# Two down projections as seven half products in three slices, with eight modulation rows made in the mixers before them

## The reference

```python
D_MODEL = 1024; SEQ = 256; D_FF = 2816

def _swiglu(xn, w_gate, w_up, w_down):
    g = jnp.einsum('bsd,df->bsf', xn, w_gate)
    up = jnp.einsum('bsd,df->bsf', xn, w_up)
    return jnp.einsum('bsf,fd->bsd', jax.nn.silu(g) * up, w_down)

# first block, for each layer
h = _swiglu(_rmsnorm(x, pre_ffn_g[layer]), ffn_w_gate[layer], ffn_w_up[layer], ffn_w_down[layer])
x = x + _rmsnorm(h, post_ffn_g[layer])

# second block, layer l: twelve rows of 512 columns each, of which the first four
# (shift and scale of the first norm) are in layer 0 also wanted for the context's condition
m = jnp.split(silu_c @ w_ada[l] + b_ada[l], 6, axis=-1)
csh1, csc1, cg1, csh2, csc2, cg2 = jnp.split(silu_cc @ w_ada[l] + b_ada[l], 6, axis=-1)
```

## Time and profile before

| | us |
|---|---|
| median of three runs | 1881.2 (1881.18 to 1881.66) |
| profiled execution, its own time | 1880.99 |
| its span, first to last instruction | 1879.2 |
| granted TensorE clock, mean | 0.992 |
| TensorE busy | 1821.9 (97%) |
| VectorE busy | 657.0 (35%) |
| ScalarE busy | 376.0 (20%) |

### The profile page before, as it was taken

One profiled execution on the slowest core, in us unless ns is written; L12 is line 12 of the kernel. 1 busy time (PEld: TensorE's weight loads), 2 busy tenths in 40 slices (PEclk: granted clock), 3 DMA queues, 4 the chain that ended last, 5 costly groups with the idle time before them and its releaser, 6 DMA issues.

```text
span 1879.2 us, 24366 instructions
## 1 busy us (share of the span) xinstructions
PE 1821.9 (97%) x10194; PEld 1200.2 (64%) x10196; DVE 657.0 (35%) x1353; ACT 376.0 (20%) x831; POOL 15.4 (1%) x31
## 2 busy tenths in 40 slices
PE   8999999999999999999999998999999999998998
PEld 7799988857999888575444433335885444433333
DVE  3278876432678653533111110112233111110112
ACT  3441110322311103423211110112013211111111
POOL 1000000000000100000000000000000000000000
PEclk9999999999999999999999999999999999999999
DMA  9744686732356883349999999999568999999996
GB/s 301 241 179 171 272 336 286 293 121 90 135 234 258 336 327 141 129 177 343 427 426 423 434 429 432 434 425 425 225 235 308 420 427 423 432 433 430 432 427 265
DMA packets 54323, 595.81 MB, mean 317 GB/s; under 512 B 6096, under 2 KB 20688, under 8 KB 24656
## 3 DMA queue, kind: packets, MB, share of 16 engines
q1 hardware_dynamic: 53648, 592.29, 76.9%
q10 hardware_dynamic: 576, 2.10, 0.3%
HBM read 588.90 MB, written 1.05 MB: 314 GB/s over the span
## 4 chain that ended last, share of the span: by engine, by line
PE 77%; DMA 19%; DVE 3%; ACT 1%; issue 0%; SPq 0%; DVEq 0%; ACTq 0%
PE ps L1357 18%; DMA ring<-in_w_up 17%; PE ps L568 16%; PE ps L870 8%; PE ps L785 7%; PE ps L1487 7%; PE ps L1312 3%; DMA ring<-in_w_ff_up 2%; PE ps L1305 2%; PE ps L638 2%; PE ps L924 1%; PE ps L727 1%; PE ps L656 1%; PE ps L670 1%; PE ps L1126 1%; PE ps L1086 1%
## 5 line engine op out<-in xcount | busy, mean ns | idle before, releaser
L1357 PE MATMUL ps<-ring,work 128*64 128x512 f32 x1792 | 405.8, 607 | 34.9 <-DMA ring<-in_w_up 29.6
L1357 PEld LDWEIGHTS ps<-ring,work 128*64 128x64 f32 x1792 | 128.8, 140 | 300.3 <-issue 248.2
L1804 ACT ACTIVATE work<-ps 128x512 f32<-128x512 f32 (+1 forms) x167 | 87.9, 532 | 696.2 <-PE ps L1487 248.7
L568 PE MATMUL ps<-hsq,ring 128*128 128x256 f32 x1024 | 225.1, 381 | 0.8 <-DVE hsq L2270 0.8
L568 PEld LDWEIGHTS ps<-hsq,ring 128*128 128x128 f32 x1024 | 193.9, 190 | 28.6 <-issue 2.8
L1487 PE MATMUL ps<-ring,work 128*64 128x512 f32 x864 | 191.6, 596 | 0.3
L2847 DVE TENSOR_TENSOR work<-ps,work 128x512 f32<-128x512 f32 x26 | 18.0, 691 | 389.2 <-ACT work L1804 389.2
L870 PE MATMUL ps<-work,ring 128*128 128x256 f32 (+1 forms) x704 | 149.5, 374 | 0.0
L2215 DVE SCALAR_TENSOR_TENSOR work<-ring,silu_c,work 128x512 f32<-128x512 f32 x196 | 143.7, 754 | 4.8
L870 PEld LDWEIGHTS ps<-work,ring 128*128 128x128 f32 x704 | 130.3, 190 | 20.7 <-issue 4.2
L1487 PEld LDWEIGHTS ps<-ring,work 128*64 128x64 f32 x864 | 59.6, 137 | 115.7 <-issue 113.9
(11 more groups left out here) (347 smaller groups left out, 1617.9 us busy)
## 6 DMA issues: line engine op xcount, KB each, us to landing
ring<-in_w_up SPq DMA_DIRECT2D x16, 4096.0 KB, 22.0
ring<-in_w_down SPq DMA_DIRECT2D x16, 4096.0 KB, 20.4
ring<-in_w_gate SPq DMA_DIRECT2D x16, 4096.0 KB, 21.4
ring<-in_w_ada SPq DMA_DIRECT2D x24, 2048.0 KB, 11.1
ring<-in_w_gate SPq DMA_DIRECT2D x24, 2048.0 KB, 11.5
ring<-in_w_up SPq DMA_DIRECT2D x22, 2048.0 KB, 14.4
ring<-in_w_down SPq DMA_DIRECT2D x20, 2048.0 KB, 14.8
ring<-in_w_ff_gate SPq DMA_DIRECT2D x10, 2048.0 KB, 13.1
```

The lines of the kernel that those rows point to most:

```text
L568: last = mm(ps[:, b, 0:T], w[:, k, m * P:(m + 1) * P], rhs[:, k, :], start=(i == 0), stop=(i == nk - 1))
L1357: last = mm(ps[e * CAP:(e + 1) * CAP, w, :], xg[:, k, e * CAP:(e + 1) * CAP], tile_of(first, w, i, 2 * k // KT, e, k % HTL), start=(k == 0 ...
L1804: return nc.scalar.activation(out_, in_, f, bias=bias, scale=scale, **kw)
```

## The change

Down becomes a copy of the scheme of gate and up, with K cut at row 1408 (11 tiles each side), tokens at 128 and output columns at 512. K's eleven pairs of tiles are taken in three slices of 4, 4 and 3 (`DOWN_SLICES`). In each slice seven products of nk x 4 matmuls of 128 x 128 (`down_slice`) are added to seven banks that stay open over all slices; VectorE makes four sums of tokens and four of weights for each slice, and in the last slice `join_down` adds the open banks into each other, so that each of the four output quarters ends in one bank. The last quarter gets one more product: identity times the quarter of columns 512 to 1023 and tokens 128 to 255, which ScalarE has copied to `h`. Each quarter (128 x 512 in one bank) is squared and copied by one instruction each, and the squares of four tiles are added by one reduction on VectorE.

The eight rows for shift and scale (four chunks, both conditions) leave the feed-forwards: two chunks are loaded and worked on in the first mixer and two in the mLSTM mixer (`pair_part`), and lie in `spare` until TensorE sums them behind the seam of the next feed-forward. Eleven rows stay in the first feed-forward and nine in the second. Groups on TensorE: 4 before and 4 now in the first feed-forward, 3 and 4 in the second, and four transposes more there. Since `spare` is now in use to the end of down, the constants are loaded after it.

```diff
+DOWN_SLICES = (4, 4, 3)
+SECOND_K = FT // 2
+UNITS = len(FAST) + len(DOWN_SLICES)
+ORDERS = dict(gate=("P1", "P5", "P6", "P2", "P7", "P3", "P4"), down=("P6", "P7", "P5", "P4", "P1", "P2", "P3"),
+              last=("P1", "P6", "P7", "P2", "P4", "P5", "P3"))
+DOWN_BANKS = dict(P1=1, P2=2, P3=6, P4=0, P5=3, P6=5, P7=4)
+PAIRS = ((0, 1), (2, 3))
+PAIR_PLACES = (0, 512, 5248, 5760)
+ADA_ROWS = (tuple((0, c) for c in range(4, 12)) + ((1, 0), (1, 1), (1, 2)), tuple((1, c) for c in range(3, 12)))
 ADA_LOADS = ((), (0, 1), (2,), (3, 4), (5,), (6,))
-ADA_IN_DOWN = 7
-ADA_ORDER = ((4, 5, 6, 7, 8, 9, 10, 11, 0, 1, 2, 3), tuple(range(12)))
+ADA_IN_DOWN = (((7, 8), (9, 10), ()), ((7, 8), (), ()))
...
+        pair_chunk(PAIRS[0][0])
+        second_out = len(chunks)
         chunk(a["ab_w_out"][1])
+        pair_chunk(PAIRS[0][1])
+        ab_last = len(chunks) - 1
...
+            for s, n in enumerate(DOWN_SLICES):
+                two = {}
+                for c in (1, 0):
+                    two[c] = len(chunks)
+                    chunk(a["w_ff_down"][l, s, c, :, 0:2 * n, :], nk=2 * n)
+                down_chunks[l].append((two[0], two[1]))
+                for i in ADA_IN_DOWN[l][s]:
+                    ada_chunk(i)
...
+            if c in (1, 3):
+                pair_chunk(PAIRS[1][c // 2])
...
+                if s < len(DOWN_SLICES) - 1:
+                    if s == 0:
+                        turn.take(S["hidden"], HTL)
+                        pe.wait_ge(S["quarter_read"], 12 * (l + 1))
+                    sums_by(4, 2)
+                    add("P6", summed(1), tokens[1])
+                    sums_by(6, 3)
+                    add("P7", plain(wb, 0), tokens[2])
+                    add("P5", summed(0), tokens[0])
+                    pe.wait_ge(S["tokens_summed"], tokens_by(l, s) + 4)
+                    add("P4", plain(wb, nk), tokens[3])
+                    release(nb, S["quarter_product"])
+                    add("P1", plain(wa, 0), low[:, :, half(0)])
+                    add("P2", plain(wa, nk), high[:, :, half(0)])
+                    pe.wait_ge(S["weights_summed"], 8 * u + 8)
+                    add("P3", summed(2), high[:, :, half(1)])
+                    release(na, S["quarter_product"])
+                    return
+
+                joins = joins_before(l, FAST.stop)
+                turn.take(S["hidden"], FT - FAST.stop * HTL)
+                add("P1", plain(wa, 0), low[:, :, half(0)])
+                sums_by(4, 2)
+                add("P6", summed(1), tokens[1])
+                made_group(l, 2)
+                sums_by(6, 3)
+                add("P7", plain(wb, 0), tokens[2])
+                pe.wait_ge(S["quarters_joined"], joins + 1)
+                add("P2", plain(wa, nk), high[:, :, half(0)])
+                owner[DOWN_BANKS["P6"]] = owner[DOWN_BANKS["P7"]] = (S["quarters_joined"], joins + 2)
+                state["stat"] = 1
+                ada_turned(ADA_COPIES[l])
+                pe.wait_ge(S["quarters_joined"], joins + 2)
+                sums_by(8, 4)
+                add("P4", plain(wb, nk), tokens[3])
+                for n in (na, nb):
+                    release(n, S["quarter_product"])
+                pe.wait_ge(S["quarters_joined"], joins + 3)
+                add("P5", summed(0), tokens[0], None if l else lambda: sum_stats(half(0)))
+                pe.wait_ge(S["quarters_joined"], joins + 4)
+                add("P3", summed(2), high[:, :, half(1)], ended=False)
+                owner[DOWN_BANKS["P1"]] = (S["seeded"], seeds_before(l, FAST.stop) + 1)
+                for name in ("P2", "P4", "P5"):
+                    hold(DOWN_BANKS[name], S["proj_copied"])
+                pe.wait_ge(S["proj_copied"], freed[S["proj_copied"]])
+                turn.give(mm(ps[:, DOWN_BANKS["P3"], :].rearrange("p (m t) -> p m t", m=4), ident, h[:, 4:KT, half(1)], start=False,
+                             stop=True, skip_group_check=True), S["quarter_product"])
+                hold(DOWN_BANKS["P3"], S["proj_copied"])
...
+                    sum_stats()
+                down_slice(l, 0)
+                made_group(l, 1)
+                down_slice(l, 1)
+                down_slice(l, 2)
+                state["chunk"] = max(down_chunks[l][-1]) + 1
...
-            seam_chunk(*next_chunk())
-            pe.wait_ge(consts_loaded, 16 * 8)
+            seam_chunk(*next_chunk(), late=4)
             freed[S["mq"]] = HTL
             dense(h, tiles_act, S["mq"], S["h_ready"], spare=True)
+            pe.wait_ge(consts_loaded, 16 * 8)
...
-                if n == TAPS_SLOT + 1:
+                if n == ab_last + 1:
                     sp.wait_ge(S["lru_conv"], HTL)
                     spread_groups(rep_glu, cpad, REP, S["glu"], taps_spread)
-                if n == 8:
+                if n == ab_last + 2:
                     sp.dma_start(rw[:], a["router_w"]).then_inc(consts_loaded, 16)
+                load(n)
                 for l in range(2):
-                    if n == max(down_chunks[l]) + 1:
-                        sp.wait_ge(S["quarter_product"], 4 * QUARTERS * (l + 1))
+                    if n == max(down_chunks[l][-1]) + 6:
+                        sp.wait_ge(S["quarter_product"], UNITS * QUARTERS * (l + 1))
                         sp.dma_start(spare[:, FRONT], a["spare_front"]).then_inc(consts_loaded, 16)
                         sp.dma_start(spare[:, BACK], a["spare_back"]).then_inc(consts_loaded, 16)
-                load(n)
-                if n == ffn_last + RING:
-                    sp.dma_start(v_rows, a["v_rows"]).then_inc(vec_loaded, 16)
+                        if l == 0:
+                            sp.dma_start(v_rows, a["v_rows"]).then_inc(vec_loaded, 16)
...
+            pair_part(0, 0, 0)
+            pair_part(0, 0, 1)
             turn.take(S["lru_conv"], HTL)
             turn.take(S["lru_gate"], 2 * HTL)
             step(V.tensor_tensor(bx[:], bx[:], xr[:], ALU.mult))
+            pair_part(0, 1, 0)
...
+            pair_part(0, 1, 1)
...
+            def down_tokens(l, s):
+
+                u, nk = slice_unit(l, s), DOWN_SLICES[s]
+                ks = slice(HTL * s, HTL * s + nk)
+                low, high = ff[:, ks], ff[:, SECOND_K + ks.start:SECOND_K + ks.stop]
+                to = [sum_tokens[:, j, 0:nk] for j in range(4)]
+                if s == len(DOWN_SLICES) - 1:
+                    to[0] = last_tokens
+                parts = ((low[:, :, half(1)], low[:, :, half(0)], "P5"), (high[:, :, half(1)], to[0], "P6"),
+                         (high[:, :, half(1)], low[:, :, half(1)], "P7"), (high[:, :, half(0)], to[1], "P4"))
+                for j, (in0, in1, read_by) in enumerate(parts):
+                    dve.wait_ge(S["quarter_product"], product_done(u - 1, read_by))
+                    step(V.tensor_tensor(to[j], in0, in1, ALU.subtract), S["tokens_summed"])
...
+            def down_plus(l, s):
+
+                n = down_chunks[l][s][1]
+                dve.wait_ge(slot_loaded[n % RING], landed(n))
+                dve.wait_ge(S["quarter_product"], product_done(slice_unit(l, s) - 1, "P5"))
+                for w in range(2):
+                    (_, (w21, w22)), sums = down_blocks(l, s, w)
+                    turn.give(V.tensor_tensor(sums[0], w21, w22, ALU.add), S["weights_summed"])
...
+            def down_second(l, s):
+
+                n, u = down_chunks[l][s][0], slice_unit(l, s)
+                dve.wait_ge(slot_loaded[n % RING], landed(n))
+                dve.wait_ge(S["quarter_product"], product_done(u - 1, "P6"))
+                for w in range(2):
+                    dve.wait_ge(S["weights_summed"], 8 * u + 1 + w)
+                    ((w11, _), _), sums = down_blocks(l, s, w)
+                    turn.give(V.tensor_tensor(sums[1], sums[0], w11, ALU.subtract), S["weights_summed"])
...
+            def join_down(l):
+
+                u = slice_unit(l, 2)
+                banks = {name: ps[:, b, :] for name, b in DOWN_BANKS.items()}
+
+                def join(name, sums):
+
+                    dve.wait_ge(S["quarter_product"], product_done(u - 1, name))
+                    step(V.tensor_tensor(banks[name], banks[name], sums, ALU.add), S["quarters_joined"])
+
+                dve.wait_ge(S["seeded"], seeds_before(l, FAST.stop) + 1)
+                join("P2", first_sums)
+                dve.wait_ge(S["quarter_product"], product_done(u, "P6"))
+                step(V.tensor_tensor(second_sums, banks["P6"], first_sums, ALU.add))
+                dve.wait_ge(S["quarter_product"], product_done(u, "P7"))
+                step(V.tensor_tensor(third_sums, banks["P7"], second_sums, ALU.add))
+                join("P4", third_sums)
+                join("P5", third_sums)
+                step(V.tensor_tensor(second_sums, second_sums, third_sums, ALU.subtract))
+                join("P3", second_sums)
...
+                down_tokens(l, 0)
                 ada_steps(1)
+                down_plus(l, 0)
```

(73 more changed lines are left out.)

382 lines of the change are left out of this document (235 added, 147 removed).

## The result

The changed kernel takes 1895.0 us (median of six runs, 1889.6 to 1899.7) against 1881.6 for the kernel before on the same chip (six runs, 1881.2 to 1883.6): ratio 1.0070, 95% interval 1.0053 to 1.0086, slower. Its profiled execution took 1892.9, 2.1 under that median, with a span of 1891.1, 11.9 over the span before. TensorE is busy for 1812.7 us, 9.2 less than before, and VectorE for 737.7, 80.7 more. The single times now spread over 10 us, where before they spread over 2.4.

What follows compares the result with a forecast made beforehand. TensorE, busy 97% of the span at nearly full clock, was taken as the bound. 1881.0 - 6.0 (first down) - 4.1 (second down) + 8.3 (first mixer's wait) + 1.7 (clock) = 1880.9 us; range 1870 to 1887.

Steps and rivals of the forecast that it cites:

- The step that failed: In the sum over the whole kernel: no other operation changes in the experts' layers, so nothing was added for them.
- First mixer: Second spread lands behind three loads, at 78.0; TensorE idles 8.3 us before the long convolution, plus 1.7 for lower clock.
- First down: Down in the first feed-forward: 7.2 us saved by fewer products, less waits; net gain 6.0, between 4.2 and 7.0.
- down in 77 us: A sign to look for: first layer's down, with its groups, takes 77 us rather than 80.5.
- Second down: Down in the second feed-forward: 6.65 us saved, less a wait, one more group and tail; net 4.1, between 2.3 and 5.5.
- tail forecast: Behind the second down's last product: 0.3 us more.
- The pace: In down, matmuls with 128 moving columns take 0.2234 us each, 64 records 7.15; more than 7.3 would prove the forecast wrong.
- VectorE's rival: VectorE falls behind in down, its sums and TensorE's products waiting in turn; 5 us lost, 1886; chance 0.12.
- The rival on the other side: The lower clock lasts through the long convolution, doubling its 14.0 us: 12.3 more, so 1893.2; chance 0.10.
- The spread isn't held up: First mixer: the three loads don't delay the copies, convolution starts near 69.7; takes off 8.3 + 1.7, 1870.9; chance 0.18.
- something unseen: Whole kernel: the remaining chance, 0.03, kept for a cause that was not named.
- The signs: Forecast wrong if convolution starts before 74 or after 82, 64 down records exceed 7.3 us, or TensorE waits inside a slice.

Runs made afterwards that it cites:

- e2: The changed kernel with 16 do-nothing instructions added at the start of TensorE's program; 1888.9 us.
- e4: The kernel before the change with 247 do-nothing instructions added at the start of TensorE's program; 1911.9 us.
- e8: The kernel before the change with 260 do-nothing instructions added at the start of TensorE's program; 1906.0 us.
- e6: The changed kernel with the second spread issued ahead of the second pair chunk and second half of `ab_w_out`, plus 6 do-nothing instructions at TensorE's start; 1884.0 us.
- e7: The changed kernel with the second spread issued ahead of the second pair chunk and second half of `ab_w_out`, plus 12 do-nothing instructions at TensorE's start; 1883.8 us.
- e10: The changed kernel run again as it is, on the same chip as the cured versions; 1894.9 us.
- e1: The changed kernel with the second spread issued ahead of the second pair chunk and second half of `ab_w_out`, which change places; 1882.0 us.
- both cures: The changed kernel with the second spread issued earlier, plus 16 or 24 do-nothing instructions at TensorE's start; 1877.3 and 1876.6 us.
- e11: The changed kernel with the second spread issued ahead of the second pair chunk and second half of `ab_w_out`, plus 24 do-nothing instructions at TensorE's start; 1876.6 us.
- e3: The changed kernel with 64 do-nothing instructions (128 waits) added at the start of TensorE's program; 1889.5 us.

## Why the prediction was wrong, point by point

- **The step that failed** is a sentence of the sum: "No other operation changes in the experts' layers." It put their change at nothing. None of their operations did change, and those layers cost 8.0 us more. 6.2 of them are the late block of code (4.33) with the lower clock behind it (some 1.9: 31 records in 8.78, at the pace of 32 in 7.09 they would take 6.87): the change adds 248 matmuls to TensorE's program (its page has 494 more records), so the branch to the experts stands elsewhere in its block of code. e2, e4 and e8 show it, and e6 and e7 show the edge moving. The other 1.8, in the first layer, are partly a stall of 0.77 us at the branch itself (behind 28 records): there the branch held the sequencer for 4.9 us, in place of 3.4 to 4.0 in the eleven profiles without that stall, with a second block's load running beside its own (865.4 and 865.8); e10 repeats it with 4.8 and 0.65. That layer took 567.5 to 569.8 in the runs here, without an order that I could explain.
- The Trainium skill has the rule, "Runtime: NRT & Kernel Launch", section "Instruction fetch mechanics": code comes in blocks of 16 KiB (256 instructions), fetched in sequence, and a taken branch whose target is outside the blocks at hand has to wait for a load. The runs agree that a load moves 16 KB and that the branch waits for one (3.3 to 4.1 us in the second layer); the count of 256 they don't measure, and my reckoning with it was 8 instructions off. They refine the rule for this kernel: the branch's own wait cost TensorE nothing in the kernel before, as queued matmuls covered it; with the edge of a block 2 to 14 instructions behind the target 4.1 to 5.5 us were lost.
- **First mixer:** forecast +8.3 idle and +1.7 clock, measured 9.47 and 1.56, +11.1 in all. The mechanism was right in the main (the start at 79.6 is inside the bounds 76.0 to 80.4; the third load landed at 68.0 where 66.2 was forecast, and the last copy 11.5 behind it, where 11.8 was). VectorE's first pair work ended at 64.3, ahead of the 67 that the forecast named.
- **First down:** forecast a net gain of 6.0, measured 5.2 to the end of down and 1.1 given back in the seam, 4.1. The chunk landed 12.85 after the slots came free (273.55 - 260.70; forecast 12.5), and the wait was 1.59 (forecast 1.0). The seam was mis-sized: I had 0.2 to 0.5 for the larger quarters, and its wait ahead of 357.90 alone is 0.86. The sign "down in 77 us" didn't fit the forecast's own sum, which gives 74.5; from the end of the plain product (260.70 + 13.81) to 349.51 it is 75.0.
- **Second down:** forecast a net gain of 4.1, measured 3.9 over the stretch with the second mixer, with a wait of 1.66 (forecast 1.4). Behind it stands a wait of 0.52 where TensorE had none before (tail forecast 0.3).
- **The pace:** 64 records of down take 7.14 us (290.64 to 297.78), as in the earlier trace rows. VectorE's rival fell: the only idle stretch of TensorE between the first product of a slice and the last is under 0.3 us. TensorE never waited for the constants, though they landed at 363.4 and 731.2, not at 349 and 723; they were issued at 350 and 718.
- **The rival on the other side** named a time of 1893 that came close, by luck: the low clock cost 1.56 us, near the forecast's 1.7, and was gone by 84 us, not through the convolution; what made up the time lay among the experts. "The spread isn't held up" fell in the changed kernel; e1 made it true, and with both cures the kernel is faster than before, 1877.3 and 1876.6 against 1882.6 and 1882.0. Its gain of some 5 us comes from the two downs: in e11's profile the stretch from the end of the long convolution to the router of the first experts is 6.9 us shorter than before, and the rest together 1.3 longer.
- **Range:** 1870 to 1887 had no case for code beyond the 0.03 for something unseen, and missed 1895.0. Of the 14.1 us over the forecast 8.0 lie among the experts, 1.1 in the first mixer, 1.9 in the first down with its seam, 0.2 in the second, 0.8 in small changes elsewhere, and 2.1 between the profiled execution and the median. With the terms up to 770 us as measured (+3.1 beyond the start) the kernel would have been at 1884, inside.
- **The signs:** none of those that would have shown the forecast wrong came (convolution before 74 or after 82, 64 records over 7.3 us, a wait for VectorE inside a slice, of which there is only 0.25 us at 345.00). They watched only the places that the change touches, and the error lay elsewhere.

## What to carry to other kernels

A load moved in front of small copies in the same queue can hold up whoever waits for the copies: three loads, the last of which landed at 68.0, cost 9.47 us here, and one alone that had landed by 56.3 cost nothing (e6, e7, e11). Put it behind them, or where the queue is idle. When a change adds or removes instructions on an engine that branches, look behind the branch for an idle stretch with no releaser and for extra loads of instructions, and try a few instructions more at a place where the engine waits anyway before judging the change. Compare the spread of single times too: 10 us in place of 2 was the first sign that something other than work had changed.

## What was not expected of the hardware

- Sixteen instructions that do nothing made the kernel 6 us faster; the stall of 4.1 to 5.5 us sat behind 35, 32 and 29 records with 0, 6 and 12 added instructions.
- An instruction that waits for two semaphore values that are already met took TensorE 0.11 us: its first matmul starts at 9.59 us with 64 of them (e3) and at 29.72 with 247 (e4), 20.13 us for 183 more.
- The sixteen parts of one load landed up to 9.2 us apart (53.8 to 63.0 in e1), and whoever waits for the load waits for the last.
- Sixteen copies inside SBUF of 142 KB move at some 200 GB/s with the engines full (207 in the earlier trace rows), half of the 442 that the loads in the earlier trace rows reach: behind the last load they still needed 11.5 us.
